# Smaller and later transfers around a streamed weight queue in a one-core Strassen trunk layer

## The chip, the cores and the metric

The kernel runs on one core of one Trainium2 chip. The metric is the device time of one execution in microseconds (us). It is compared as the median of several runs. The engines are TensorE (PE in the profile, its weight loads PEld), VectorE (DVE), ScalarE (ACT), GpSimd (POOL) and the queue engine SyncE (SP). DMA transfers are asked for from two places only, SP and POOL, and all run on the core's 16 DMA engines.

## The reference

One layer of a streaming encoder over 4096 tokens of width 1024, with a memory of 256 rows. Shortened:

```
h    = rms_norm(x, pre_norm)                      # x: (1, 4096, 1024)
proj = h @ w_in                                   # 1024 -> 3072 (b, c, u) + 1536 (gate) + 512 (mq)
z    = c * u;  mix = b * conv3(z)                 # causal convolution over time, 3 taps
k, v = split(rms_norm(mem, mem_norm) @ w_mem_kv)  # 256 memory rows, 4 heads of 128
mem_o = softmax(mq @ k.T / sqrt(128)) @ v
y    = (concat([mix, mem_o]) * silu(gate)) @ w_out
out  = x + rms_norm(y, post_norm)
```

## The kernel before

All arithmetic is fp32. Each fp32 operand is split in a high and a low part, and each product is three matmuls (hi x hi, hi x lo, lo x hi; lines 1701 to 1703), each of 128x128 weights by 512 columns.

**Tiling.** The tokens are 8 tiles of 512 (`NT`), two tiles to a macro (`MACROS` = 4). In a macro TensorE goes through 20 pairs of weight blocks (`PAIRS`), and each pair is multiplied by a Strassen scheme with seven products (`PRODUCTS`, in the order R1, R5, R6, R3, R7, R2, R4). One product is a *unit*: 12 matmuls. A *step* is one product in a macro, `step = 7 * pair + r`, so a macro has 140 steps. What a pair holds is its kind: `q` (memory queries), `m` (gates of the memory branch), and groups `c`, `u`, `b`, `g` of the convolution branch. After the four macros the output projection (`OUT_STEPS`, 16 pairs) follows.

**Weights.** In macro 0 the Strassen sums of weights are built by ACT and DVE in one of four buffers (`slots`, `SLOTS` = 4) and kept in memory on the chip's HBM (`w_split`). In macros 1 to 3 SP loads each unit back (`load_unit`, line 600, 512 KB). SP goes through the steps in order, and `load_unit` for unit u waits until unit u-4 has been multiplied:

```
sp.wait_ge(unit_done, u - SLOTS + 1)
```

So what stands in SP's loop at `now = step - SLOTS` is issued when TensorE has ended a unit that is four units back. Whatever else SP asks for stands behind this load in SP's queue, and ahead of the next.

**Keys and values.** In macro 3, after steps 18, 20, ..., 32 (`KV_AT`), TensorE also multiplies eight key/value blocks, 0 to 7, of two units each. They use the same four slots, so in this stretch "four units back" is two steps and one key/value block back. SP loads a block's raw weights (`load_kv(b)`, line 645, 512 KB) in one of two buffers. In program step 17 + 2b ACT makes the high parts of block b (line 937) and DVE the low parts (line 1357), and TensorE multiplies them after step 18 + 2b.

**Stores and staging.** POOL stores what a pair has made when the whole pair is done (`keep`): queries and SiLU gates as one transfer of 1024 KB, gated convolution outputs as two of 512 KB. Tokens of the next macro come as four halves of 1024 KB (`load_x` after the pairs in `X_AFTER`). In macro 2 (`SUMS_MACRO`) POOL also brings and stores sums of the output weights: rows for the memory part (`memory_rows_in`, two transfers of 512 KB; `memory_rows_out`), and for the convolution part (`out_sums_in`, `out_sums_out`, 1024 KB each). At the end of macro 3 SP loads 1024 KB parts for the output projection (`OUT_X_AT`) and four blocks of 384 KB (`OUT_RAW_AT`).

Of the kernel before, what the change touches and what calls it, by code (L numbers as in the profile page):

```python
# [56 lines left out]
X_AFTER = {2: 0, 3: 2, 4: 1, 5: 3}  # L57
# [15 lines left out]
OUT_X_AT = [122, 123, 124, 125]  # L73
# [114 lines left out]
def trunk(nc, x, x_t, mem, mem_x, in_gains, post_g, conv, w_in, w_kv, w_conv, w_mem, out):  # L188
# [6 lines left out]
    with ExitStack() as ctx:  # L195
# [254 lines left out]
        def mix_free(eng, p, tile):  # L450

            if p == ALL_PAIRS:
                eng.wait_ge(g_kept_dma, 32 * 4 * MACROS)
            else:
                eng.wait_ge(y_final, 2 * (p - ALL_PAIRS) - 1 + tile)
# [56 lines left out]
        def zb_free(eng, p):  # L512

            m = p // PAIRS
            if kind_of(p) == "q":
                if row_of(p) > FIRST_Q:
                    eng.wait_ge(q_kept_dma, 16 * (2 * m + 1))
                elif m < MACROS - 1:
                    eng.wait_ge(tap0_done, 4 * 4 * (m + 1))
                    eng.wait_ge(halo_out, 2 * 4 * (m + 1))  # L520
                else:
                    eng.wait_ge(q_kept_dma, 16 * 2 * m)
            elif row_of(p) > FIRST_C:
                eng.wait_ge(tap0_done, 4 * conv_group(p))
                eng.wait_ge(halo_out, 2 * conv_group(p))
            elif m:
                eng.wait_ge(q_kept_dma, 16 * count("q", p))
            else:
                eng.wait_ge(m_kept_dma, 16 * 2)
# [17 lines left out]
        def load_block(eng, p, x):  # L547

            if (p, x) in WAS:
                raw_used(eng, *WAS[p, x])  # L550
            sub = 2 * (p - ALL_PAIRS) + (x in (X21, X22))
            for h in range(2):
                eng.wait_ge(mem_kept_dma[h], 16 * MH // 2 * (sub // SUB + 1))
            eng.wait_ge(g_kept_dma, 32 * 4 * (sub // (2 * SUB) + 1))
            done = raw_dma[PLACE[p, x]] if p == ALL_PAIRS else block_dma[x]
            eng.dma_start(raw(p, x), flat(g_kept[sub, 1 * (x in (X22, X12))])).then_inc(done, 16)

        @block.sync
        def _(sp):
# [87 lines left out]
            def load_q(n):  # L647
                t, h = divmod(n, MH)
                if n >= 2:
                    sp.wait_ge(q_lo_done, n - 1)  # L650
                else:
                    sp.wait_ge(mw_kept_dma[0], 16 * PRODUCTS)
                sp.wait_ge(q_kept_dma, 16 * 2 * (t // 2 + 1))
                sp.dma_start(q_raw[n % 2], q_kept[t // 2, h, t % 2]).then_inc(q_dma[n % 2], 16)

            def load_m(n):
                t, h = divmod(n, MH)
                if n >= 2:
                    sp.wait_ge(mem_gated, n - 1)
                else:  # L660
                    sp.wait_ge(w_lo, BUILT[KV_UNIT[KV_BLOCKS - 1, 1]] + 1)
                sp.wait_ge(m_kept_dma, 16 * 2 * (t // 2 + 1))
                sp.dma_start(m_raw[n % 2], m_kept[t // 2, h, t % 2]).then_inc(m_dma[n % 2], 16)

            for m in range(1, MACROS):
                for i in range(PAIRS):
                    p = m * PAIRS + i
                    for r in range(PRODUCTS):
# [15 lines left out]
                        if m + 1 < MACROS:  # L684
                            continue
                        if now == 2:
                            sp.wait_ge(hop_lo_done, (m + 1) * PRODUCTS)
                            sp.dma_start(mem_in[:], mem).then_inc(mem_dma, 16)
                        if now == 6:
                            sp.wait_ge(sums_kept_dma, 16 * HK)  # L690
                        if now in (6, 9):
                            load_kv((now - 6) // 3)
                        if now in (12, 14):
                            load_q((now - 12) // 2)
                        if now in KV_AT and KV_AT.index(now) + 2 < KV_BLOCKS:
                            load_kv(KV_AT.index(now) + 2)
                        if now == KV_AT[-1]:
                            load_m(0)
                            load_m(1)
# [19 lines left out]
                        if step == OUT_RAW_AT:  # L719
                            sp.wait_ge(mem_gated, HEADS)  # L720
                            sp.wait_ge(scores_done, HEADS)
                            for x in (X11, X21, X22, X12):
                                load_block(sp, ALL_PAIRS, x)
                    if i in X_AFTER and m + 1 < MACROS:
                        sp.wait_ge(hop_lo_done, (m + 1) * PRODUCTS)
                        load_x(X_AFTER[i], m + 1)
# [21 lines left out]
        def _(pool):  # L748
# [45 lines left out]
            def keep(p):  # L794
                m, i, kind = p // PAIRS, row_of(p), kind_of(p)
                if kind == "q":
                    pool.wait_ge(c12_done, seven_to(p))
                    pool.wait_ge(c22_done, seven_to(p))
                    pool.wait_ge(c11_done, seven_to(p))
                    pool.wait_ge(copied, count("qcy", p) + 1)  # L800
                    pool.dma_start(kept_as(q_kept, m, i - FIRST_Q), zb[:, :, HALO:]).then_inc(q_kept_dma, 16)
                if kind == "m":
                    pool.wait_ge(silu_done, silu_count(p, R4))
                    pool.dma_start(kept_as(m_kept, m, i), zb[:, :, HALO:] if p == 1 else mix[:]).then_inc(m_kept_dma, 16)
                if kind == "g":
                    group = (i - FIRST_C) // 4
                    pool.wait_ge(gated, 4 * (count("g", p) + 1))
                    for f in range(2):
                        pool.dma_start(g_kept[2 * SUB * m:2 * SUB * (m + 1), group // 2, :, group % 2 * 2 + f, :].rearrange("s p n -> p s n"),
                                       flat(mix[:, 2 * f:2 * f + 2, :]).rearrange("p (s n) -> p s n", n=P)).then_inc(g_kept_dma, 16)  # L810
# [7 lines left out]
            def out_sums_in(k):  # L818

                if k:  # L820
                    pool.wait_ge(sums_kept_dma, 16 * k)
                else:
                    pool.wait_ge(mw_lo, HB * PRODUCTS)
                for tile in range(2):
                    pool.dma_start(out_sums[:, 2 * tile:2 * tile + 2, :], w_conv[tile, :, k:KT:HK, :]).then_inc(out_raw_dma, 16)

            def out_sums_out(k):
                pool.wait_ge(out_sum_done, 4 * (k + 1))
                pool.dma_start(sums_kept[:, :, k, :].rearrange("s p n -> p s n"), out_sums).then_inc(sums_kept_dma, 16)

            def memory_rows_in(k):
# [5 lines left out]
                for tile in range(2):  # L837
                    pool.dma_start(out_sums[:, 2 * tile:2 * tile + 2, :], w_mem[tile, :, k:MH:HB, :]).then_inc(mw_raw_dma, 16)
# [5 lines left out]
            for p in range((MACROS - 1) * PAIRS):  # L844
                m, i = divmod(p, PAIRS)
                if m == SUMS_MACRO and i == 0:
                    memory_rows_in(0)
                for step in range(PRODUCTS * i, PRODUCTS * (i + 1)):
                    if m == SUMS_MACRO and step in MW_AT:
                        memory_rows_out(MW_AT.index(step))  # L850
                        if MW_AT.index(step) == PRODUCTS - 1:
                            memory_rows_in(1)
                    rows(m, step)
                keep(p)
                if m == SUMS_MACRO and i in SUMS_AFTER:
                    k = SUMS_AFTER.index(i)
                    if k:
                        out_sums_out(k - 1)
                    if k < HK:
                        out_sums_in(k)  # L860
            for step in range(PAIRS * PRODUCTS):
                p, r = divmod(step, PRODUCTS)
                if r == R5 and p:
                    keep((MACROS - 1) * PAIRS + p - 1)
# [3 lines left out]
            keep(ALL_PAIRS - 1)  # L868
# [37 lines left out]
        def _(act):  # L906
# [78 lines left out]
            def evacuate(p, r):  # L985
# [37 lines left out]
                if kind in "mg" and r in (R3, R7, R2, R4):  # L1023
                    if kind == "m":
                        if r == R3:
                            act.wait_ge(m_kept_dma, 16 * count("m", p))
                            act.wait_ge(g_kept_dma, 32 * count("g", p))
# [208 lines left out]
        def _(dve):  # L1236
# [13 lines left out]
            def norm(tile, k):  # L1250
                if tile < 2:
                    dve.wait_ge(spread_done, tile + 1)
                else:
                    dve.wait_ge(rs_wide_dma, 16 * (tile - 1))
                    dve.wait_ge(x_dma[tile % 2 + 2 * (k // HK)], 16 * (tile // 2 + 1))
# [185 lines left out]
            def convolve(p, n):  # L1441
# [16 lines left out]
                if n == 0:  # L1458
                    if group % 4 == 0:
                        dve.wait_ge(m_kept_dma, 16 * count("m", p))  # L1460
                    if group:
                        dve.wait_ge(g_kept_dma, 32 * group)
# [62 lines left out]
            def memory(p, r, step):  # L1525
                if 13 <= step < 15:
                    dve.wait_ge(rs_wide_dma, 16 * (NT - 1))
                    dve.wait_ge(mem_dma, 16)
# [402 lines left out]
```

## Time and profile before

| | |
|---|---|
| median of three runs | 2178.57 us (2177.86 to 2178.81) |
| the profiled execution | 2178.16 us, its span 2176.3 us |
| TensorE (PE) busy | 2152.8 us, 99% |
| VectorE busy | 1209.7 us, 56% |
| ScalarE busy | 745.6 us, 34% |
| GpSimd busy | 174.7 us, 8% |
| DMA | 550.33 MB, mean 253 GB/s |

The profiled execution takes 1.9 us more than its span, and lies 0.4 us below the median of the three runs. By time, macro 0 runs to about 398 us, macro 1 to about 790, macro 2 to about 1185, macro 3 to about 1706, and the output projection to the end. Busy shares say that TensorE is the engine that matters; what is left to find is in its waits.

### The profile page before, as it was taken

How to read it: one execution, taken by the hardware profiler on the slowest of the kernel's cores; microseconds unless marked ns; L12 is line 12 of the kernel's file. 1: busy time of each engine (PE TensorE's matmuls, PEld its weight loads, DVE VectorE, ACT ScalarE, POOL GpSimd, SP SyncE). 2: the span in 40 equal slices, each digit the busy share in tenths (PEclk: the TensorE clock that was granted, in tenths of full speed). 3: DMA queues.
4: the chain of work that ended last, by engine and by line, in shares of the span. 5: the costliest groups of instructions: out<-in, count | busy, mean ns of one | idle time of the engine just before them, and what ended most of it. 6: DMA issues, size and time to landing. Idle time of an engine off the chain costs nothing.

```text
span 2176.3 us, 26536 instructions
## 1 busy us (share of the span) xinstructions
PE 2152.8 (99%) x9820; PEld 1782.1 (82%) x9820; DVE 1209.7 (56%) x1819; ACT 745.6 (34%) x1312; POOL 174.7 (8%) x285
## 2 busy tenths in 40 slices
PE   8999999999999999999999999999999999999998
PEld 7888888888888888788887888888887788888887
DVE  7668767643335353354345237576764755566665
ACT  5444333411221342221123233545351633333333
POOL 0000000000000000111100000101010111111110
PEclk9999999999999999999999999999999999999999
DMA  6897777678766778987877765656667866666665
GB/s 242 306 339 277 274 268 269 244 252 274 243 217 217 267 263 307 335 287 265 295 233 257 247 226 190 223 193 218 198 204 291 337 252 240 238 232 227 247 228 193
DMA packets 157103, 550.33 MB, mean 253 GB/s; under 512 B 18032, under 2 KB 18064, under 8 KB 153904
## 3 DMA queue, kind: packets, MB, share of 16 engines
q1 hardware_dynamic: 122048, 416.34, 54.9%
q0 software_dynamic: 34928, 132.30, 17.3%
q8 instruction: 79, 1.29, 0.2%
q14 instruction: 48, 0.39, 0.1%
HBM read 404.90 MB, written 143.67 MB: 252 GB/s over the span
## 4 chain that ended last, share of the span: by engine, by line
PE 89%; DMA 4%; DVE 4%; ACT 1%; issue 1%; SPq 0%; DVEq 0%; ACTq 0%
PE banks L1701 29%; PE banks L1703 29%; PE banks L1702 29%; DMA slots<-w_split 3%; PE banks L1818 1%; DVE hop_lo L1307 1%; DVE x_in L1275 1%; ACT hop_hi L983 1%; ACT probs L1074 0%; DMA mw_stream<-mw_kept 0%; DMA raws<-in_w_in 0%; DMA raws<-in_w_kv 0%; DVE rmax L1483 0%; DVE pt_lo L1498 0%; DVE mix L1467 0%
## 5 line engine op out<-in xcount | busy, mean ns | idle before, releaser
L1701 PE MATMUL banks<-hop_hi,slots 128*128 128x512 f32 x2184 | 853.1, 391 | 8.3 <-DMA slots<-w_split 8.0
L1702 PE MATMUL banks<-hop_lo,slots 128*128 128x512 f32 x2184 | 850.4, 389 | 0.0
L1703 PE MATMUL banks<-hop_hi,slots 128*128 128x512 f32 x2184 | 850.0, 389 | 0.0
L1701 PEld LDWEIGHTS banks<-hop_hi,slots 128*128 128x128 f32 x2184 | 410.1, 188 | 97.3 <-DMA slots<-w_split 13.2
L1703 PEld LDWEIGHTS banks<-hop_hi,slots 128*128 128x128 f32 x2184 | 409.9, 188 | 86.1
L1702 PEld LDWEIGHTS banks<-hop_lo,slots 128*128 128x128 f32 x2184 | 410.1, 188 | 83.1
L1703 PE MATMUL banks<-hop_hi,out_slot 128*128 128x512 f32 x448 | 175.4, 392 | 0.0
L1701 PE MATMUL banks<-hop_hi,out_slot 128*128 128x512 f32 x448 | 175.3, 391 | 0.0
L1702 PE MATMUL banks<-hop_lo,out_slot 128*128 128x512 f32 x448 | 175.2, 391 | 0.0
L1357 DVE TENSOR_TENSOR out_slot<-out_raws,out_slot 128x768 fp32r<-128x768 f32 x112 | 107.3, 958 | 90.3 <-ACT out_slot L937 90.3
L1414 DVE TENSOR_TENSOR u<-banks,u 128x512 f32<-128x512 f32 x54 | 37.3, 691 | 210.5 <-PE banks L1703 210.5
L937 ACT ACTIVATE out_slot<-out_raws 128x768 fp32r<-128x768 f32 x112 | 94.3, 842 | 147.1 <-PE banks L1703 80.4
L1008 ACT ACTIVATE s<-banks 128x512 f32<-128x512 f32 x78 | 46.7, 598 | 263.1 <-PE banks L1703 263.1
L1357 DVE TENSOR_TENSOR slots<-raws,slots 128x512 fp32r<-128x512 f32 x76 | 51.7, 690 | 85.8 <-ACT slots L937 85.8
L1702 PEld LDWEIGHTS banks<-hop_lo,out_slot 128*128 128x128 f32 x448 | 84.1, 188 | 18.6
L1701 PEld LDWEIGHTS banks<-hop_hi,out_slot 128*128 128x128 f32 x448 | 84.1, 188 | 18.7 <-DVE out_slot L1357 0.3
L1703 PEld LDWEIGHTS banks<-hop_hi,out_slot 128*128 128x128 f32 x448 | 84.1, 188 | 18.5
L1016 ACT ACTIVATE u<-banks 128x512 f32<-128x512 f32 x78 | 46.6, 598 | 134.2 <-PE banks L1703 134.2
L1012 ACT ACTIVATE p<-banks 128x512 f32<-128x512 f32 x78 | 46.6, 598 | 124.5 <-PE banks L1703 124.5
L1307 DVE TENSOR_TENSOR hop_lo<-x_in,hop_hi 128x2048 fp32r<-128x2048 f32 x29 | 66.0, 2290 | 27.2 <-ACT hop_hi L983 27.1
L937 ACT ACTIVATE slots<-st_w 128x512 fp32r<-128x512 f32 x80 | 50.1, 626 | 70.6 <-PE banks L1703 51.3
L1357 DVE TENSOR_TENSOR slots<-st_w,slots 128x512 fp32r<-128x512 f32 x80 | 55.1, 689 | 30.9 <-ACT slots L937 30.5
(188 smaller groups left out, 2602.1 us busy)
## 6 DMA issues: line engine op xcount, KB each, us to landing
slots<-w_split SPq DMA_DIRECT2D x406, 512.0 KB, 4.2
w_split<-slots SPq DMA_DIRECT2D x140, 512.0 KB, 3.5
mw_stream<-mw_kept SPq DMA_DIRECT2D x96, 512.0 KB, 4.5
out_raws<-g_kept POOLq DMA_DIRECT2D x60, 384.0 KB, 6.1
raws<-in_w_in SPq DMA_DIRECT2D x86, 256.0 KB, 4.5
x_in<-in_x_t SPq DMA_DIRECT2D x16, 1024.0 KB, 8.2
g_kept<-mix POOLq DMA_DIRECT2D x32, 512.0 KB, 6.9
x_res<-in_x POOLq DMA_DIRECT2D x32, 512.0 KB, 5.3
```

Of the source, the lines that this page charges most:

```text
L937: nc.scalar.activation(dst, src, ACT.Copy).then_inc(w_hi, 1)
L983: nc.scalar.activation(hop_hi[:, r, :, :], (OUT_OF if m == OUT else Y_OF)[r], ACT.Copy).then_inc(hop_hi_done, 1)
L1008: nc.scalar.activation(temp(p, R2), a, ACT.Copy).then_inc(s1_done, 1)
L1012: nc.scalar.activation(temp(p, R7), bank_x, ACT.Copy).then_inc(p5_done, 1)
L1016: nc.scalar.activation(temp(p, R3), a, ACT.Copy).then_inc(u2_done, 1)
L1275: nc.vector.tensor_tensor(dst, a, b, ALU.subtract).then_inc(t_made, 1)
L1307: nc.vector.tensor_tensor(hop_lo[:, r, :, :], (OUT_OF if m == OUT else Y_OF)[r], hop_hi[:, r, :, :].bitcast(f32), ALU.subtract).then_inc(h ...
L1357: nc.vector.tensor_tensor(lo, src, hi.bitcast(f32), ALU.subtract).then_inc(w_lo, 1)
L1414: nc.vector.tensor_tensor(dst, src, temp(p, r), ALU.add).then_inc(done, 1)
L1701: nc.tensor.matmul(dst, a, c, start=first, stop=False, skip_group_check=True)
L1702: nc.tensor.matmul(dst, a, d, start=False, stop=False, skip_group_check=True)
L1703: return nc.tensor.matmul(dst, b, c, start=False, stop=last, skip_group_check=True)
```

## The change

Every transfer that was made in one or two large parts is made in smaller ones, and several are asked for at other steps:

- `keep` becomes `keep_block`: queries, gates and outputs are stored block by block (256 KB each) as soon as a block is ready. The counts in waits on these stores go from 16 or 32 to 64 a pair.
- Tokens come as 16 quarters of 256 KB, one every fourth step from step 16 to step 76 (`X_QUARTERS`), instead of four halves.
- The memory input comes as four parts at `now` = 7 to 10 instead of one at `now` = 2.
- Key/value blocks 0 and 1 are asked for at `now` = 11 and 13 instead of 6 and 9, and each of the others one `now` later than before.
- The first memory rows are asked for at the end of macro 1 (`ROWS_AT`) and each pair of such transfers is split over two steps. Sums are stored in four parts.
- The parts for the output projection are asked for at steps 122, 124, 127 and 131 (before 122 to 125), and its four blocks at 126, 129, 133 and 135 (before all at 127).

The diff, cut to its core:

```
-X_AFTER = {2: 0, 3: 2, 4: 1, 5: 3}
+X_QUARTERS = {16 + 4 * q: ((0, 2, 1, 3)[q // HK], q % HK) for q in range(4 * HK)}
-OUT_X_AT = [122, 123, 124, 125]
+OUT_X_AT = [122, 124, 127, 131]
+OUT_BLOCKS_AT = [126, 129, 133, 135]
-SUMS_AT = [PRODUCTS * i + 13 for i in SUMS_AFTER[:HK]]
+SUMS_AT = [PRODUCTS * i + 15 for i in SUMS_AFTER[:HK]]
+ROWS_AT = [127, 131]
-OUT_RAW_AT = 127
+MEM_AT = (7, 8, 9, 10)
...
+            def load_x_quarter(n, q, m):
+                tile, k = n % 2, n // 2 * HK + q
+                sp.dma_start(x_in[:, tile, k, :], x_t[2 * m + tile][:, k, :]).then_inc(x_dma[n], 16)
...
-                if r == R4 and p in X_AFTER:
+                if PRODUCTS * p + r in X_QUARTERS:
                     sp.wait_ge(hop_lo_done, PRODUCTS)
-                    load_x(X_AFTER[p], 1)
+                    load_x_quarter(*X_QUARTERS[PRODUCTS * p + r], 1)
...
-                        if now == 2:
+                        if now in MEM_AT:
                             sp.wait_ge(hop_lo_done, (m + 1) * PRODUCTS)
-                            sp.dma_start(mem_in[:], mem).then_inc(mem_dma, 16)
-                        if now == 6:
-                            sp.wait_ge(sums_kept_dma, 16 * HK)
-                        if now in (6, 9):
-                            load_kv((now - 6) // 3)
+                            two = slice(2 * MEM_AT.index(now), 2 * MEM_AT.index(now) + 2)
+                            sp.dma_start(mem_in[:, two, :], mem[:, two, :]).then_inc(mem_dma, 16)
+                        if now == 11:
+                            sp.wait_ge(sums_kept_dma, 64 * HK)
+                        if now in (11, 13):
+                            load_kv((now - 11) // 2)
...
-                        if now in KV_AT and KV_AT.index(now) + 2 < KV_BLOCKS:
-                            load_kv(KV_AT.index(now) + 2)
-                        if now == KV_AT[-1]:
+                        if now - 1 in KV_AT and KV_AT.index(now - 1) + 2 < KV_BLOCKS:
+                            load_kv(KV_AT.index(now - 1) + 2)
+                        if now - 1 == KV_AT[-1]:
                             load_m(0)
                             load_m(1)
...
+            def keep_block(p, r):
+
+                m, i, kind, n = p // PAIRS, row_of(p), kind_of(p), OF[r]
+                f, t = divmod(n, 2)
                 if kind == "q":
...
+                    pool.dma_start(q_kept[m, 2 * (i - FIRST_Q) + f, t], zb[:, n, HALO:]).then_inc(q_kept_dma, 16)
```

On SP, in the key/value stage of macro 3, the rows before are these (`st_w<-q_kept` are the first two query loads, `slots<-w_split` the streamed units, `raws<-in_w_kv` key/value blocks; the first one here is block 2):

```order
L654 DMA st_w<-q_kept 128x512
L600 DMA slots<-w_split 128x1024 x4
L645 DMA raws<-in_w_kv 128x1024
L600 DMA slots<-w_split 128x1024 x2
L645 DMA raws<-in_w_kv 128x1024
```

and now:

```order
L660 DMA st_w<-q_kept 128x512
L606 DMA slots<-w_split 128x1024 x5
L651 DMA raws<-in_w_kv 128x1024
L606 DMA slots<-w_split 128x1024 x2
L651 DMA raws<-in_w_kv 128x1024
```

Block 2 stands behind five streamed units since the query load instead of four, and the later blocks keep this shift, since two units stand between each two of them in both.

On POOL, at the change from macro 1 to macro 2, the rows before are these (`in_w_mem` are the memory rows, `row` the token rows for the norm):

```order
L801 DMA q_kept<-zb 128x4x512 x2
L838 DMA raws<-in_w_mem 128x2x512 x2
L804 DMA m_kept<-mix 128x4x512 x2
L764 DMA row<-in_x 128x1024
L842 DMA mw_kept<-mw_split_98 128x1024
```

and now:

```order
L859 DMA raws<-in_w_mem 128x2x512
L809 DMA q_kept<-zb 128x512 x2
L859 DMA raws<-in_w_mem 128x2x512
L809 DMA q_kept<-zb 128x512 x6
L812 DMA m_kept<-mix 128x512 x8
L770 DMA row<-in_x 128x1024
```

The memory rows moved ahead of nearly all query stores, and a store of 1024 KB became four.

On POOL, in the middle of macro 2 (the seventh memory row leaves, the second set comes in), the rows before:

```order
L842 DMA mw_kept<-mw_split_99 128x1024
L842 DMA mw_kept<-mw_split_98 128x1024
L838 DMA raws<-in_w_mem 128x2x512 x2
L764 DMA row<-in_x 128x1024
L842 DMA mw_kept<-mw_split_99 128x1024
```

and now:

```order
L863 DMA mw_kept<-mw_split_99 128x1024
L863 DMA mw_kept<-mw_split_98 128x1024
L859 DMA raws<-in_w_mem 128x2x512 x2
L770 DMA row<-in_x 128x1024
L863 DMA mw_kept<-mw_split_99 128x1024
```

Here the order is the same: the two steps between the halves hold no other work of POOL.

## Rows read from the trace of the kernel before

**Rows 1.** The page, busy time of each engine.

```profile
PE 2152.8 (99%) x9820; PEld 1782.1 (82%) x9820; DVE 1209.7 (56%) x1819; ACT 745.6 (34%) x1312; POOL 174.7 (8%) x285
```

**Rows 2.** Waits of PE: us in total, times, longest.

```profile
PE banks L1701 <- DMA slots<-w_split: 8.0, 9, 1.6
...
PE banks L1701 <- DMA mw_stream<-mw_kept: 0.9, 1, 0.9
```

**Rows 3.** Waits of PE in macro 2, 790 to 1185 us.

```profile
PE banks L1701 <- DMA slots<-w_split: 4.5, 5, 1.6
```

**Rows 4.** Waits of PE early in macro 3, 1185 to 1300 us.

```profile
PE banks L1701 <- DMA slots<-w_split: 2.0, 2, 1.5
PE banks L1701 <- DVE slots L1357: 1.1, 2, 0.9
```

**Rows 5.** Waits of PE at the end of macro 3, 1660 to 1706 us.

```profile
PE banks L1701 <- DMA slots<-w_split: 1.5, 2, 0.7
```

**Rows 6.** Chain that ended last, 780 to 900 us: start, us, what.

```profile
789.39 9.38 DMA slots<-w_split
...
889.22 8.14 DMA slots<-w_split
```

**Rows 7.** Timeline of POOL, 784 to 792 us: start, us, engine, line.

```profile
787.97 0.75 POOL L801 DMA_DIRECT2D q_kept<-zb  x1 [18.42 <-DVE zb L1414]
788.71 1.42 POOL L838 DMA_DIRECT2D raws<-in_w_mem  x2
```

**Rows 8.** Timeline of POOL, 884 to 890 us.

```profile
886.18 0.53 POOL L842 DMA_DIRECT2D mw_kept<-mw_split  x1 [6.90 <-DVE mw_split L1302]
886.71 1.45 POOL L838 DMA_DIRECT2D raws<-in_w_mem  x2
```

**Rows 9.** Waits of the SP queue, 1180 to 1190 us.

```profile
SPq L688 <- DVE hop_lo L1307: 5.8, 1, 5.8
```

**Rows 10.** Timeline of SP in the key/value stage, 1236 to 1245.6 us.

```profile
1236.18 0.32 SPq L600 DMA_DIRECT2D slots<-w_split  x1
1236.55 0.43 SPq L645 DMA_DIRECT2D raws<-in_w_kv  x1
1242.10 3.04 SPq L600 DMA_DIRECT2D slots<-w_split  x2
1245.18 0.43 SPq L645 DMA_DIRECT2D raws<-in_w_kv  x1
```

**Rows 11.** Timeline of PE, 1244.3 to 1244.9 us: the start of block 2.

```profile
1244.40 0.39 PE L1703 MATMUL banks<-hop_hi,slots 128*128 128x512 f32 x1
1244.62 0.28 PE L1701 MATMUL banks<-mem_hi,slots 128*128 128x256 f32 x1
```

**Rows 12.** DMA to landing: four key/value blocks (1236 to 1262 us); all streamed units.

```profile
DMA to landing us min/median/max: 4.1/5.1/5.7
...
DMA to landing us min/median/max: 2.6/4.1/10.2
```

**Rows 13.** Chain that ended last, 1262 to 1280 us: block 6.

```profile
1270.33 8.04 DMA raws<-in_w_kv
1278.40 0.64 ACT slots L937
1279.06 0.70 DVE slots L1357
1279.81 0.50 PE banks L1701
```

**Rows 14.** Stretches at the end: busy us (x) by engine, PEclk, DMA share, GB/s.

```profile
2170.50:2174.00 3.50, 0.00 (x0) 0.00 (x0) 2.86 (x5) 0.85 (x3) 0.54 (x1) 1.00 0.39 156
2174.00:2176.30 2.30, 0.00 (x0) 0.00 (x0) 0.00 (x0) 0.00 (x0) 0.00 (x0) 0.50 0.60 223
```

**Rows 15.** The stretch 1664 to 1672 us, columns as in rows 14.

```profile
1664.00:1672.00 8.00, 7.25 (x31) 5.66 (x31) 6.13 (x14) 0.60 (x1) 0.00 (x0) 1.00 1.03 406
```

**Rows 16.** Timelines of SP and DVE in macro 0, 56 to 75 us.

```profile
58.56 1.36 SPq L565 DMA_DIRECT2D raws<-in_w_in  x2
...
64.71 2.29 DVE L1307 TENSOR_TENSOR hop_lo<-x_in,hop_hi 128x2048 fp32r<-128x2048 f32 x1 [2.13 <-ACT hop_hi L983]
...
73.76 0.68 DVE L1351 TENSOR_TENSOR st_w<-raws 128x512 f32<-128x512 f32 x1
```

More of the change, by code:

```diff
@@ L718, in _ @@
                             load_stream(0, R5)
-                        if step == OUT_RAW_AT:
+                        if step in OUT_BLOCKS_AT:
                             sp.wait_ge(mem_gated, HEADS)
                             sp.wait_ge(scores_done, HEADS)
[L722 to L726, printed above, removed]
+                            load_block(sp, ALL_PAIRS, (X11, X21, X22, X12)[OUT_BLOCKS_AT.index(step)])
             for r in (R6, R3, R7, R2, R4):
@@ L808, in keep @@
-                    for f in range(2):
-                        pool.dma_start(g_kept[2 * SUB * m:2 * SUB * (m + 1), group // 2, :, group % 2 * 2 + f, :].rearrange("s p n -> p s n"),
-                                       flat(mix[:, 2 * f:2 * f + 2, :]).rearrange("p (s n) -> p s n", n=P)).then_inc(g_kept_dma, 16)
+                    pool.wait_ge(gated, 4 * count("g", p) + ORDER_OF[r])
+                    pool.dma_start(g_kept[SUB * (2 * m + t):SUB * (2 * m + t + 1), group // 2, :, group % 2 * 2 + f, :].rearrange("s p n -> p s n"),
+                                   mix[:, n, :].rearrange("p (s n) -> p s n", n=P)).then_inc(g_kept_dma, 16)
@@ L812, in keep_gated, with keep_first, keep @@
+            def keep_first(p):
+                for r in (R3, R7, R2, R4):
+                    keep_block(p, r)
+            def keep(p, r):
+                if p >= DIRECT and kind_of(p) in "qm" and r in (R3, R7, R2, R4):
+                    keep_block(p, r)
+                if kind_of(p) == "g" and r in (R7, R2, R4):
+                    keep_block(p, {R7: R3, R2: R7, R4: R2}[r])
+                if p and kind_of(p - 1) == "g" and r == R1:
+                    keep_block(p - 1, R4)
             def keep_gated(n):
@@ L845, in _ @@
                 m, i = divmod(p, PAIRS)
[L846 to L848 removed]
+                for r in range(PRODUCTS):
+                    step = PRODUCTS * i + r
+                    if m + 1 == SUMS_MACRO and step in ROWS_AT:
+                        memory_rows_in(0, ROWS_AT.index(step))
                     if m == SUMS_MACRO and step in MW_AT:
                         memory_rows_out(MW_AT.index(step))
[L851 to L852 removed]
+                    for tile in range(2):
+                        if m == SUMS_MACRO and step == MW_AT[PRODUCTS - 1] + 2 * tile:
+                            memory_rows_in(1, tile)
                     rows(m, step)
[L854 to L860, printed above, removed]
+                    keep(p, r)
+                    if m == SUMS_MACRO and i - 1 in SUMS_AFTER[:HK] and r in (R6, R7):
+                        out_sums_in(SUMS_AFTER.index(i - 1), int(r == R7))
+                    if m == SUMS_MACRO:
+                        for k, first in enumerate(SUMS_AT):
+                            if first < step <= first + 4:
+                                out_sums_out(k, step - first - 1)
+                if p < DIRECT:
+                    keep_first(p)
             for step in range(PAIRS * PRODUCTS):
                 p, r = divmod(step, PRODUCTS)
[L863 to L864 removed]
+                keep((MACROS - 1) * PAIRS + p, r)
                 for n in range(HEADS):
@@ L1459, in convolve @@
                     if group % 4 == 0:
-                        dve.wait_ge(m_kept_dma, 16 * count("m", p))
+                        dve.wait_ge(m_kept_dma, 64 * count("m", p))
                     if group:
-                        dve.wait_ge(g_kept_dma, 32 * group)
+                        dve.wait_ge(g_kept_dma, 64 * group)
                 w = conv_w[:, j, :]
```

64 lines of the change are left out of this document (31 added, 33 removed).

## The prediction

> **What bounds the kernel now.** I read the busy times first [rows 1]: TensorE is busy for 2152.8 of 2176.3 us, so no transfer matters until it makes TensorE wait, and everything that could be won is 23.5 us. Next I read TensorE's waits [rows 2]: the only large group is on streamed units that landed late, nine times and 8.0 us. By stretches, five of these (4.5 us) are in macro 2, two (2.0 us) early in macro 3 with two waits on key/value parts (1.1 us) beside them, and two (1.5 us) at the end of macro 3 [rows 3 to 5]. Macros 0 and 1 have none. A wait costs a little more than its idle time: SP's loads follow the units, and two of them start 3.04 - 0.32 = 2.72 us apart [rows 10], so 12 matmuls take 2.72 us, 0.23 each, while the view draws each 0.39 long [rows 11]. So 0.16 us goes on top of each idle time. The nine waits cost about 8.0 + 9 x 0.16 = 9.4 us.
>
> Then the chain shows what a wait is made of. A streamed unit is asked for when the unit four back has ended, so it has three units, 3 x 2.72 = 8.16 us, to land. In most cases it takes 4.1 us; in the two cases of [rows 6] it took 9.38 and 8.14. The first was asked for at 789.39, just behind a 1024 KB query store and with two 512 KB memory rows [rows 7]. So the waits are bursts: about 2 MB of other transfers asked for within two microseconds.
>
> **The change part by part.**
>
> Stores block by block, tokens in quarters, memory rows earlier. In macro 2 the five waits cost 4.5 + 5 x 0.16 = 5.3 us. The burst at 788 us comes apart: its memory rows go ahead of the query stores, a step or more apart, and each store is a quarter of what it was. I count its wait as gone, and those behind the other large stores and the 1024 KB token halves too. One burst stays whole: at 886 us a memory row leaves and two 512 KB parts come in behind it [rows 8]. Nothing stands between the two parts in POOL's order, so splitting them over two steps does not part them. The unit asked for behind them took 8.14 us [rows 6]. I leave 1.0 us for this and for what stays near 956 us (one of the two sum loads is still asked for there), so this part gives 4.3 us, between 3 and 5.3.
>
> The price of more transfers: POOL gets 24 + 24 + 32 + 12 = 92 more (queries 8 to 32, gates 8 to 32, gated outputs 32 to 64, sums 4 to 16). At no more than the 0.75 us that the 1024 KB store took [rows 7] that is 69 us more on an engine that is busy for 174.7 [rows 1] and idle around them: nothing on the path.
>
> Here a rule speaks against the change. The trace has 1024 KB stores ahead of the worst landings [rows 6, 7]. The Trainium skill, "DMA: Bandwidth & Descriptors", section Bandwidth, says to batch transfers to at least 1 MiB; it gives 341 GB/s at 1 MB and 138 at 64 KB. By it each part of 256 KB would hold the DMA engines longer per byte, and the gain above would be eaten in part. By the rows it is not the engines' time but the size of a burst that makes a unit late, and the sum goes by that.
>
> The memory input at `now` = 7 to 10. Before, SP stood at `now` = 2 for 5.8 us until the last operand of the macro was split [rows 9], and the next streamed unit was asked for late. At `now` = 7 the operand is long done. This wait goes, and so, I count, does the other of the two early in macro 3, where a gate store of 1024 KB was under way: 2.0 + 2 x 0.16 = 2.3 us.
>
> The output parts at 122, 124, 127, 131. Four transfers of 1024 KB behind four units of 512 KB asked for 1.5 MB per 2.72 us, 560 GB/s, where the DMA engines moved 406 at full share [rows 15]. Spaced by two or more units it is 375 GB/s or less. I take 1.6 of the 1.5 + 2 x 0.16 = 1.8 us.
>
> In macro 0 the first quarter (step 16) puts SP behind the last operand of the macro: that operand's low part ends at 67.0 us, and two raw weight parts that SP asked for at 58.56 and after stand behind the wait [rows 16]. They would be asked for at about 67.9 and land some 4.5 us later, at 72.4; the sum that reads raw weights runs at 73.76 [rows 16]. It is covered by about one microsecond, and TensorE is four units behind that sum. Nothing; at worst 2 us.
>
> **The key/value blocks, which cost.** Blocks 2 to 7 are asked for one streamed unit later. In SP's order block 2 stands behind five units instead of four. Before, SP asked for it at 1236.55, at the end of step 20; TensorE then had block 1, step 21 and step 22 ahead, and began block 2 at 1244.62 [rows 10, 11]. The next streamed unit was asked for at 1242.10, when step 21 ended. The block now stands behind that one: 1242.10 + 0.36 = 1242.46 (the distance of the two issues before, 1236.18 and 1236.55). That leaves 1244.62 - 1242.46 = 2.16 us. It needs its landing plus the way through ACT and DVE: for block 6 from the landing at 1270.33 + 8.04 = 1278.37 to TensorE at 1279.81, 1.44 us [rows 13]. So TensorE waits for
>
> landing + 1.44 - 2.16 = landing - 0.72 us, once for each block.
>
> Four of these blocks landed in 4.1 to 5.7 us, median 5.1 [rows 12]. In the new place there is less in the queue: the streamed unit before last was asked for 5.9 us earlier and not 2.7 us [rows 10], and the gate stores beside them are quarters. I take 4.3, near the shortest. Each block waits 3.6 us. Six blocks have this place (blocks 0 and 1 are asked for five steps or more ahead): 6 x 3.6 = 21.6 us, between 6 x 3.4 = 20.4 (landing 4.1) and 6 x 4.4 = 26.4 (landing 5.1). In exchange the two waits on key/value parts go, 1.1 + 2 x 0.16 = 1.4 us. Queued behind the waiting conversions are ACT's and DVE's readings of the next unit's bank; they run while the block itself is multiplied, about 3 us (1242.10 - 1236.18 - 2.72 = 3.2, a short wait included [rows 10]), and add nothing.
>
> **The sum**, against the profiled execution: 2178.16 - 4.3 - 2.3 - 1.6 - 1.4 + 21.6 = 2190.2. The median of the runs was 0.4 above the profiled one: 2190.5 us. That is 0.55% slower; a measurement of this kernel can tell about 0.2%, 4.4 us.
>
> **The rivals.**
>
> - *Faster: the later request is hidden.* If the blocks landed in time, only the gains are left: 2178.6 - 9.6 = 2169.0 us. For the sum to break even a block may wait 9.6 / 6 = 1.6 us, so it would have to land in 2.3 us. The shortest landing of all 406 streamed units of this size was 2.6 [rows 12], and a block has one of them right ahead of it. Chance 5%, half of it for the middle (about 2178).
> - *The waits also cost clock.* TensorE stands for more than 3 us six times. At the end of the kernel its granted clock was still full for 3.5 us without a matmul, and half after that [rows 14]; a wait of 3.6 is at that edge, one of 4.4 beyond it. If after each wait the block's own 3 us ran at 1.2 instead of 2.4 GHz, that is 6 x 3 = 18 us more: 2208. The Trainium skill, "TensorE: Matmul & The Clock Gate", Part 1, says that the clock falls to 1.2 GHz after an idle window; by that rule waits of this length may each fall on either side. Chance 8% that it costs most of this, and some of it is in the upper end of the range.
> - *The gains do not come.* The small transfers make as much wait in macro 2 as the large ones (the 886 us burst grows, the rest only moves), and the blocks land in 5.1 us. 2178.6 + 26.4 - 4 = 2201. Chance 10%; half gains, 2195, is within my range.
> - *The change moves nothing that counts*, 2178: it would need both the blocks hidden and the bursts unchanged. 2%.
>
> **How the numbers follow.** The forecast, 2187 to 2196, has 75%. Low end: landing 4.1, all of 5.3 + 2.3 + 1.8 + 1.4 gained, 2178.6 + 20.4 - 10.8 = 2188; a landing of 3.8 takes off 1.8: 2186. High end: landing 5.1 and 5 us of gains give 2200. Range 2186 to 2200. Faster by over 0.2%: 3%. Within: 4%. Slower: 93%.
>
> **What would show it.** Right: TensorE waits on VectorE's parts of key/value blocks (the two waits of 1.1 us become about six of 3.4 us idle, 20 us), the blocks asked for right behind the first streamed unit after a block, waits on streamed units down from nine to three or four, SP's 5.8 us gone, none of the 9 us landings. Wrong: key/value blocks asked for before step 21 ends or landing in under 3 us; new waits on streamed units; a granted clock below full in macro 3; or TensorE waiting in macro 0.

## The result, and the profile after

The changed kernel takes 2204.26 us (2203.04 to 2204.91, four runs) where the kernel before takes 2178.25 beside it: a ratio of 1.0111, with a 95% interval of 1.0091 to 1.0131. It is 26 us slower. The sign was forecast, the size was not: the forecast was 12 us (2190.5, at most 2200). Two executions of versions further down, one of 5618 us and one of 3086 us, were in a slower state and are left out of the medians.

The waits of TensorE in the changed kernel (line, what was waited for, us in total, times, longest), which answer to [rows 2]:

```profile
PE banks L1725 <- DVE slots L1381: 22.0, 6, 4.1
...
PE banks L1725 <- DMA slots<-w_split: 3.0, 4, 1.4
...
PE banks L1725 <- DMA mw_stream<-mw_kept: 1.6, 1, 1.6
```

Six new waits on VectorE's half of a key/value block, 22.0 us idle, stand where two of 1.1 us stood [rows 4]. Counted from the start of the last matmul before to the start of the first after, less the 0.23 us that lie between any two, they are 23.0 us; this is what "from start to start" means below. Waits on streamed units went from nine to four and from 8.0 to 3.0 us. So the waits account for some 15 us of loss, and 26 were measured. The rest is in the granted clock. Stretches around the first of the new waits (us, busy us and instructions by engine, PEclk, DMA share, GB/s):

```profile
1242.60:1246.50 3.90, 0.00 (x0) 0.00 (x0) 0.71 (x2) 1.37 (x3) 0.00 (x0) 1.00 0.71 285
1246.60:1247.10 0.50, 0.47 (x4) 0.50 (x5) 0.49 (x1) 0.16 (x1) 0.00 (x0) 1.00 0.00 0
1247.20:1250.50 3.30, 3.30 (x18) 3.30 (x17) 0.00 (x0) 0.00 (x0) 0.00 (x0) 0.50 0.00 0
1250.60:1256.20 5.60, 5.60 (x28) 4.73 (x28) 0.42 (x1) 0.98 (x2) 0.00 (x0) 1.00 0.20 61
```

TensorE stood for 3.9 us at full clock (2.4 GHz), worked for half a microsecond, and only then got half the clock (1.2 GHz) for 3.3 us, in which it did 18 matmuls of 256 columns (the clock is the column behind the engines, 1.00 for full and 0.50 for half). Over the whole stage, the same columns for both kernels, before and after:

```profile
1225.00:1330.00 105.00, 103.36 (x531) 87.16 (x530) 42.61 (x79) 35.46 (x80) 3.01 (x4) 1.00 0.62 209
```

```profile
1225.00:1360.00 135.00, 112.56 (x526) 93.91 (x527) 42.22 (x79) 35.53 (x81) 5.32 (x9) 0.92 0.47 162
```

In the changed kernel about the same number of matmuls took 30 us more, and the mean clock over 135 us was 0.92: 0.08 x 135 = about 11 us of full-speed work were not granted (the clock is rounded to a hundredth; matmul by matmul it is 9.7, below). This view prices the clock without following a single matmul. It must not be added to the busy column, which already contains it: busy time rose from 103.4 to 112.6 us for as many matmuls, which is the same loss seen from the other side.

How a block came to be late, from the chain of the changed kernel at the first of the six (start, us, what):

```profile
1239.86 0.32 SPq L606
1240.22 4.88 DMA raws<-in_w_kv
1245.13 0.64 ACT slots L961
1245.79 0.70 DVE slots L1381
```

The request is 0.36 us behind the streamed unit's, as forecast; it landed in 4.9 us (the six: 4.3 to 4.9), and TensorE started at 1246.63. Landing - 0.72 gives 4.2 us, and 4.24 is the distance above the regular one from the last matmul before to the first after.

The same matmul in both traces shows where the time goes: the changed kernel is 1.9 us behind at 45 us, 2.1 behind at 790, 2.7 *ahead* at 1220, 28.5 behind at 1310, 26.1 at 1706, and 26.8 at the end. So macro 2 and the start of macro 3 gained 4.8 us, the end of macro 3 gained 2.4, the output projection lost 0.7, and the key/value stage lost 31.2.

### The profile page after: what moved, and what is told of

Read it like the earlier page. It is cut to its first block, busy times and chain, and to the rows that moved or that the text cites. A ratio compares the mean times of both kernels' runs of the same rounds, so it can differ in the third digit from the quotient of the medians.

```text
span 2203.1 us, 26654 instructions
## 1 busy us (share of the span) xinstructions
PE 2162.8 (98%) x9820; PEld 1792.1 (81%) x9820; DVE 1209.7 (55%) x1819; ACT 747.1 (34%) x1312; POOL 223.0 (10%) x377
## 4 chain that ended last, share of the span: by engine, by line
PE 91%; DMA 4%; DVE 3%; ACT 1%; issue 1%; SPq 0%; DVEq 0%; ACTq 0%
PE banks L1725 30%; PE banks L1727 30%; PE banks L1726 30%; DMA slots<-w_split 2%; DMA raws<-in_w_kv 1%; PE banks L1842 1%; DVE hop_lo L1331 1%; DMA mw_stream<-mw_kept 0%; ACT probs L1098 0%; DMA raws<-in_w_in 0%; DVE rmax L1507 0%; DVE x_in L1299 0%; DVE pt_lo L1522 0%; DVE slots L1381 0%; ACT hop_hi L1007 0%
## 5 line engine op out<-in xcount | busy, mean ns | idle before, releaser
L816 POOL DMA_DIRECT2D g_kept<-mix x64 | 48.4, 758 | 426.6 <-DVE mix L1463 424.0
```

Source lines behind the costliest of these rows:

```text
L816: pool.dma_start(g_kept[SUB * (2 * m + t):SUB * (2 * m + t + 1), group // 2, :, group % 2 * 2 + f, :].rearrange("s p n -> p s n"), mix[:, ...
```

## Experiments: is it the key/value request, and is it the clock?

**One thing undone.** Everything of the change stays, only blocks 2 to 7 are asked for as before.

```
-                        if now - 1 in KV_AT and KV_AT.index(now - 1) + 2 < KV_BLOCKS:
-                            load_kv(KV_AT.index(now - 1) + 2)
+                        if now in KV_AT and KV_AT.index(now) + 2 < KV_BLOCKS:
+                            load_kv(KV_AT.index(now) + 2)
```

> The changed kernel with one thing undone: key/value blocks 2 to 7 are asked for at the step at which the kernel before asks for them. Theory A (the later request is the whole loss: six waits that cost 23.0 us and, after each, a stretch at half clock worth about 1.6 us, and all else in the change gains about 5 us): the six waits and the low clock in macro 3 go, and the time is 2171 to 2174 us, below the kernel before. Rival B (the many small transfers cost time too, and the key/value waits only hide it): 2178 us or more. Rival C (the low clock comes from something else in the change): the clock still falls in macro 3, and the time is about 2182.

Measured: 2171.15 us, ratio 0.9966 (0.9953 to 0.9979), 7 us below the kernel before and 33 below the changed one. In its waits none on a key/value block is left, and the clock in the stage is full (the stretch 1225 to 1330 us below). One stretch at half clock is left elsewhere in this trace, at 1713 us behind a wait of 1.8 us for the first streamed memory rows.

```profile
1225.00:1330.00 105.00, 104.73 (x535) 88.37 (x534) 47.80 (x93) 36.55 (x83) 5.52 (x9) 1.00 0.62 208
```

One request, one step later, turned a version that is faster by 0.3% into one that is slower by 1.1%.

**The one thing alone.** The kernel before with only the two lines of the opposite edit.

```
-                        if now in KV_AT and KV_AT.index(now) + 2 < KV_BLOCKS:
-                            load_kv(KV_AT.index(now) + 2)
+                        if now - 1 in KV_AT and KV_AT.index(now - 1) + 2 < KV_BLOCKS:
+                            load_kv(KV_AT.index(now - 1) + 2)
```

> The kernel before with only the later request for key/value blocks 2 to 7. Theory A: six waits near 3.8 us and six stretches at half clock, 2178.3 + 23 + 9.7 - 1.4 (two short waits replaced) = 2209.6 us. Rival B: part of the 31 us in this stretch needs the other edits, so it is under 2203. With the gate stores still at 1024 KB two of the six waits should be longer by a microsecond or so.

Measured: 2209.30 us, ratio 1.0160 (1.0125 to 1.0195), against 2209.6 expected. The six waits and the clock of 0.92 are there:

```profile
1225.00:1360.00 135.00, 112.45 (x524) 93.58 (x523) 41.09 (x74) 34.15 (x73) 3.00 (x4) 0.92 0.46 160
```

By the same matmuls its stage lost 30.8 us, where the changed kernel's lost 31.2; its trace also lost 1.7 us at the start, in code that this edit does not touch, and had one more stretch at half clock, behind a streamed unit at 887 us. So the agreement to 0.3 us is in part luck; that of the stage is not. Of its six waits two are longer than in the changed kernel (4.3 and 4.0 against 4.0 and 3.7), the others equal or a little shorter, none by the microsecond that was expected with the large gate stores. The small stores are not what set the landing.

**Filling the waits.** The changed kernel with work of no use on TensorE in front of each late block. The added matmuls write a free bank, and nothing reads them.

```
                         if step in KV_AT:
+                            if KV_AT.index(step) >= 2:
+                                for _ in range(13):
+                                    nc.tensor.matmul(psum[:, 4, :], hop_hi[:, R3, 0, 0:P], hop_hi[:, R3, 0, :], start=True, stop=True)
                             keys_values(KV_AT.index(step))
```

> The changed kernel with 13 more matmuls (2.9 us, into a free bank, results unused) on TensorE just before it waits for each of key/value blocks 2 to 7. They fit in the waits, so the blocks start no later. If the waits alone set the time, it stays at 2204. Theory A: TensorE idles under 1 us each time, the clock stays full, and the six stretches at half clock, 9.7 us in all, are given back: about 2194.5 us. If the half clock has no price it stays at 2204.

Measured: 2196.64 us, ratio 1.0090 (1.0066 to 1.0115): 78 matmuls more, 7.6 us less. The blocks start as late as ever: with the added matmuls left out, the six distances from start to start are 22.7 us, against 23.0. What is given back is clock. Its stage:

```profile
1225.00:1345.00 120.00, 115.69 (x578) 96.38 (x577) 37.60 (x70) 32.27 (x70) 5.51 (x10) 1.00 0.50 173
```

By the medians 2 us of the 9.7 expected did not come, but in the stage all of it did: by the same matmuls the stage lost 21.2 us here and 31.2 in the changed kernel, 10.0 less. So the 2 us lie outside the stage, and where is not shown: the profiled execution is the longest of the four (2208.5 us) and lost 13 us in the output projection, so it doesn't stand for the others there.

**A shorter real wait.** The changed kernel with the late block asked for in front of the streamed unit of that moment.

```
+                            early = step - SLOTS - 1
+                            if m + 1 == MACROS and early in KV_AT and KV_AT.index(early) + 2 < KV_BLOCKS:
+                                sp.wait_ge(unit_done, UNIT_OF[p, r] - SLOTS + 1)
+                                load_kv(KV_AT.index(early) + 2)
                             load_unit(p, r)
...
-                        if now - 1 in KV_AT and KV_AT.index(now - 1) + 2 < KV_BLOCKS:
-                            load_kv(KV_AT.index(now - 1) + 2)
```

> The changed kernel, blocks 2 to 7 still asked for when the step after the block two before has ended, but ahead of the streamed unit of that moment instead of behind it. Each block lands sooner by the 0.36 us of the issue and about 1.3 us of 512 KB not in front of it, so a wait is about 2.2 us instead of 3.8. Theory A (the clock falls for the long wait, not for the fact of waiting): it stays full, and the time is 2204.3 - 9.7 - 6 x 1.6 = about 2185 us. If the clock falls all the same, about 2195. If the landing does not depend on what stands in front of it in the queue, 2202 or more.

Measured: 2190.63 us, ratio 1.0054 (1.0039 to 1.0069), between the forecast of theory A (2185) and the case that the clock falls all the same (2195). The waits:

```profile
PE banks L1727 <- DVE slots L1383: 14.1, 6, 2.4
```

Six waits of 2.4 to 2.6 us from start to start: the blocks landed in 3.5 to 3.7 us instead of 4.3 to 4.9, and were asked for 0.4 us sooner. But the clock did not stay full, nor did it always fall. The first two of these waits and what came after each:

```profile
1240.30:1242.40 2.10, 0.00 (x0) 0.00 (x0) 0.65 (x2) 1.31 (x3) 0.00 (x0) 1.00 1.01 398
1243.10:1246.40 3.30, 3.30 (x18) 3.30 (x17) 0.00 (x0) 0.00 (x0) 0.00 (x0) 0.50 0.01 4
1252.70:1254.80 2.10, 0.00 (x0) 0.00 (x0) 0.65 (x2) 1.15 (x2) 0.00 (x0) 1.00 1.03 419
1255.00:1258.00 3.00, 3.00 (x25) 3.00 (x26) 1.04 (x2) 0.63 (x1) 0.54 (x1) 1.00 0.13 51
```

Two waits of the same length, one followed by 18 matmuls in 3.3 us at half clock and one by 25 in 3.0 at full. Three of the six were followed by such a stretch. The sum closes with it: 7.9 us less waiting and about half of the clock's loss, 13 us, against the 13.6 measured (13.1 in the stage by the same matmuls). Theory A was wrong on this point: it is not only the long wait that costs clock.

**The same idle time, made by filling.** Six instead of 13 added matmuls in the changed kernel.

```
-                                for _ in range(13):
+                                for _ in range(6):
```

> The changed kernel with 6 more matmuls (1.36 us) before the wait for each of key/value blocks 2 to 7 instead of 13. TensorE then stands 2.2 to 2.9 us each time, as in the version that asked for the blocks ahead of the streamed unit, where three of six such waits were followed by a stretch at half clock; the blocks start as late as in the changed kernel. Theory (the clock falls by how long TensorE has just stood and when, not by how late the block is): two to four stretches at half clock in macro 3 instead of six, 2204.3 - 2 to 4 x 1.6 = 2198 to 2201 us. Rival (any wait that the changed kernel has is enough): six, 2204.

Measured: 2203.67 us, ratio 1.0107 (1.0072 to 1.0141): as slow as the changed kernel, nearer to the rival than to the theory. Its profiled execution is the fastest of the four at 2199.57, with four stretches at half clock in the stage; by the same matmuls it lost 27.2 us in the stage, 4.0 less than the changed kernel. Its mean clock over the run was 0.996, that of the other three 0.994, which is also where the changed kernel lies with its six in the stage and one at the start. So it is likely that these three lost clock more often than four times; how often, and where, is not shown.

**The shorter wait, filled.** The version with the block in front, and 8 added matmuls.

```
+                            if KV_AT.index(step) >= 2:
+                                for _ in range(8):
+                                    nc.tensor.matmul(psum[:, 4, :], hop_hi[:, R3, 0, 0:P], hop_hi[:, R3, 0, :], start=True, stop=True)
```

> The version that asks for blocks 2 to 7 ahead of the streamed unit, with 8 more matmuls (1.8 us) before each block. The waits of about 2.5 us shrink to 0.7 us for TensorE. Theory: no stretch at half clock in macro 3, three times 1.6 us given back: 2190.6 - 4.8 = 2185.8 us. Rival (the half clock there came from elsewhere): 2190.6.

Measured: 2186.74 us, ratio 1.0027 (1.0009 to 1.0045), where 2185.8 was expected on a chip on which the kernel before ran 1.5 us slower (2179.87). No stretch at half clock is left in the stage, which lost 13.8 us by the same matmuls, where the version without the added ones lost 18.1:

```profile
1225.00:1335.00 110.00, 106.39 (x532) 88.67 (x531) 35.16 (x65) 31.86 (x69) 5.20 (x9) 1.00 0.52 183
```

## Experiments: where the gain of the rest comes from

Each of these is the kernel before with one part of the change. On this chip the kernel before ran at 2180.32 us, spread from 2175 to 2190, so one or two microseconds can't be told by the clock on the wall; the waits can.

**Stores block by block** (`keep` replaced by `keep_block`, counts of 16 and 32 replaced by 64):

```
-                    pool.dma_start(kept_as(q_kept, m, i - FIRST_Q), zb[:, :, HALO:]).then_inc(q_kept_dma, 16)
+                    pool.dma_start(q_kept[m, 2 * (i - FIRST_Q) + f, t], zb[:, n, HALO:]).then_inc(q_kept_dma, 16)
```

> The kernel before with only the stores of queries, gates and gated outputs made block by block (256 KB instead of 1024 or 512 KB). Theory A (a unit is late when about 2 MB of other transfers is asked for at once): of the waits on streamed units those behind a query or gate store (789, 829 us) and behind a gated output store with other transfers (1064 us) go or shrink below 0.5 us, about 2.5 us gained, and the wait of 1.1 us on key/value block 6, asked for behind a 1024 KB gate store, goes too: about 2174.5 us. Rival (more and smaller transfers cost as much as they save): 2178 or more.

Measured: 2177.29 us, ratio 0.9984 (0.9967 to 1.0001), which can't decide between the two. The waits can, for theory A: those in macro 2 went from 4.5 [rows 3] to 1.9 us, and on block 6 one of 0.2 us is left; the view of macro 2, then of 1185 to 1300 us:

```profile
PE banks L1717 <- DMA slots<-w_split: 1.9, 3, 1.1
```

```profile
PE banks L1717 <- DMA slots<-w_split: 2.4, 1, 2.4
PE banks L1717 <- DVE slots L1373: 0.2, 1, 0.2
```

The second view also shows a loss: SP's stand for the memory input, not part of this edit, now costs 2.4 us idle instead of 1.5, and a stretch at half clock followed it at 1193 us.

**Tokens in quarters** (`X_QUARTERS` and `load_x_quarter`):

```
-X_AFTER = {2: 0, 3: 2, 4: 1, 5: 3}
+X_QUARTERS = {16 + 4 * q: ((0, 2, 1, 3)[q // HK], q % HK) for q in range(4 * HK)}
```

> The kernel before with only the tokens asked for in 16 quarters instead of four halves. Theory A: the longest wait of macro 2 (1.8 us, the unit asked for at 876 us right behind a 1024 KB half) goes, the others stay: 2176 to 2177 us. The macro 0 wait of SP for its first quarter costs TensorE nothing. Rival: the quarters only spread the same lateness over more units, no change, 2178.

Measured: 2176.96 us, ratio 0.9987 (0.9971 to 1.0004). The wait behind the token half (1.8 us at 884 us) is gone, smaller ones remain, 2.1 us idle in place of 4.5:

```profile
PE banks L1705 <- DMA slots<-w_split: 2.1, 5, 0.6
```

**Loads for the output projection apart** (`OUT_X_AT`, `OUT_BLOCKS_AT`):

```
-OUT_X_AT = [122, 123, 124, 125]
+OUT_X_AT = [122, 124, 127, 131]
+OUT_BLOCKS_AT = [126, 129, 133, 135]
```

> The kernel before with only the spacing of the loads for the output projection at the end of macro 3. Theory A: the two waits at 1667 and 1673 us go, 1.8 us or a little more: about 2176 us. Rival: the last of these loads now runs beside those of the next stage, and the first streamed memory rows of the output projection come later: the wait there grows from 1.1 us by as much, no gain.

Measured: 2177.60 us, ratio 0.9982 (0.9963 to 1.0001). No wait of TensorE is left between 1660 and 1706 us, against 1.5 us in [rows 5], and the same matmul at 1706 us is 2.4 us earlier relative to 1660. The wait at the first streamed memory rows stayed at 1.1 us from start to start, so the rival fell.

**Memory input in parts, later** (`MEM_AT`):

```
-                        if now == 2:
+                        if now in MEM_AT:
```

> The kernel before with only the memory input in four parts at the later steps. Theory A: SP no longer stands 5.8 us for the last operand, the wait at 1192 us (1.6 us) goes: about 2176.7 us. Rival: the 1024 KB now compete with key/value block 1 and the query store there, and another unit is late: no change.

Measured: 2181.81 us, ratio 0.9994 (0.9976 to 1.0012), no change that can be told. Between 1185 and 1225 us there is no wait of TensorE at all, and SP no longer stands for the operand; the profiled execution is 1.8 us ahead in that stretch. The same execution lost far more, 7.6 us, in the output projection, which this edit does not touch. Differences of that size between executions are why the median says nothing about an edit worth 1.8 us.

**A better version.** The changed kernel with the request undone, and two more edits: the second half of each sum load a step earlier, and the post-norm gains asked for after the first output blocks.

```
-                    if m == SUMS_MACRO and i - 1 in SUMS_AFTER[:HK] and r in (R6, R7):
-                        out_sums_in(SUMS_AFTER.index(i - 1), int(r == R7))
+                    if m == SUMS_MACRO and i - 1 in SUMS_AFTER[:HK] and r in (R6, R3):
+                        out_sums_in(SUMS_AFTER.index(i - 1), int(r == R3))
...
-            pool.dma_start(post_gain[:], post_g).then_inc(post_dma, 16)
...
                 if j == 0:
+                    pool.dma_start(post_gain[:], post_g).then_inc(post_dma, 16)
                     load_residual(0)
```

> The changed kernel with key/value blocks asked for as before, and two more edits: the second half of each sum load one step earlier, off the token row and gated output store that made a unit 1.5 us late at 989 us, and the post-norm gains (512 KB) asked for after the first output blocks and not before them, since the first streamed memory rows of the output projection came 1.7 us late there. Theory: both waits shrink by half or more, and the stretch at half clock behind the second goes: 2168 to 2170 us. Rival (these loads only change places): 2171.

> The changed kernel with key/value blocks asked for as before, once more, to compare the last one with on the same chip and to see how far its waits in macro 2 and at the output projection vary: 2171 us.

Measured together: 2169.57 us, ratio 0.9947 (0.9930 to 0.9964), and for the version without the two edits 2170.67 us, 0.9955 (0.9939 to 0.9971). The two extra edits can't be told from nothing. In the waits the one on the first streamed memory rows is gone (it was 1.7 us from start to start in the version without them), and so is the one at 989 us (1.6 us there), but another streamed unit in macro 2, at 965 us, is now 2.0 us late, so in macro 2 the rival holds in this trace. The view of the version with them begins:

```profile
PE banks L1874 <- POOL ident L762: 3.5, 1, 3.5
PE banks L1725 <- DMA slots<-w_split: 2.5, 2, 2.0
```

Both versions beat both kernels of the case.

## Why the prediction was right in direction and wrong in size

The steps against the profiled execution: 12.0 us were forecast and 26.8 measured.

- **The late request: right, and nearly its size.** Landing - 0.72 us for each of six blocks held to the tenth (4.9 gives 4.2). The landings were 4.3 to 4.9, median 4.5, where 4.3 was taken: 23.0 us for 21.6.
- **The clock: the step that failed.** The forecast gave it nothing, on the argument that "its granted clock was still full for 3.5 us without a matmul, and half after that [rows 14]; a wait of 3.6 is at that edge". The rival with the clock got 8%, priced at 18 us, and "a granted clock below full in macro 3" stood among its signs of being wrong; that sign came. Each of the six waits was followed by half clock for 3.3 us or a little more, and the stage lost 9.7 us by the same matmuls in both traces: 31.2, less 23.0 - 1.5 of waits. The filled version lost 10.0 us less in the stage, 7.6 by the medians. The argument failed on two counts. One idle stretch at the end of a kernel shows one case: from the end of the last matmul to the fall it was 3.7 us there, 2.4 us at the end of the changed kernel, and up to 5.1 in the other traces; and within the kernel the same idle time was followed by half clock in some places and not in others. And in the changed kernel all six falls came 0.3 to 0.7 us after TensorE had begun again, so a clock that is full through the wait says nothing on what follows.
- **The price of a fall** was taken from the wrong thing, the length of the block (3 us each, 18 in all). It is the length of the stretch at half clock: 9 matmuls of 512 columns from 18.4 to 21.7 us in the changed kernel, 16 in the same stretch before, both below.

```profile
18.40:21.70 3.30, 3.30 (x16) 2.74 (x15) 3.30 (x6) 3.30 (x8) 0.00 (x0) 1.00 1.04 403
```

```profile
18.40:21.70 3.30, 3.30 (x9) 2.60 (x8) 3.30 (x6) 3.30 (x7) 0.00 (x0) 0.50 1.03 400
```

- **A term that was not in the sum: 1.9 us at the start.** These two rows lie behind a wait of 2.1 us for the first operand that both kernels have. In the changed kernel's profiled execution a stretch at half clock followed it, before none, and with the request undone none either, with all other edits in. The version with the later request alone, whose start is that of the kernel before, has it too (1.7 us). So it is not the change's: of all 14 traces four have it.
- **Macro 2 and the start of macro 3: right kind, too much in this trace.** 6.6 us were forecast (4.3 and 2.3), 4.8 came. In the other traces that have all of these edits and no others in this stretch it was 3.8 to 7.1, 6.5 with the request undone, so one trace can't tell the size of this term. The burst at 886 us stayed whole, as POOL's order said, and cost 0.8 us. What was missed is a new one: in macro 2 the second half of the first sum load, a token row, a token quarter and the block stores now stand together, and the unit asked for at 981 us was 1.5 us late. It is not late in every execution: with the request undone POOL has the same order there, and the first trace shows no such wait, the second one of 1.6 us. POOL in the changed kernel:

```profile
975.56 0.56 POOL L770 DMA_DIRECT2D row<-in_x  x1 [19.85 <-ACT row L940]
977.17 0.77 POOL L816 DMA_DIRECT2D g_kept<-mix  x1 [1.06 <-DVE mix L1463]
977.93 0.72 POOL L845 DMA_DIRECT2D raws<-in_w_conv  x1
979.88 0.79 POOL L816 DMA_DIRECT2D g_kept<-mix  x1 [1.23 <-DVE mix L1463]
981.89 1.51 POOL L816 DMA_DIRECT2D g_kept<-mix  x2 [1.22 <-issue]
```

- **The end of macro 3: right.** 1.6 us forecast; 2.4 came by the same matmuls. The 0.7 us lost at the first streamed memory rows were not forecast.
- **Macro 0: right.** SP did stand for 9.8 us at its first quarter, and TensorE lost nothing by it.
- **The rule against small transfers** did not bear on the time: POOL's busy time rose from 174.7 to 223.0 us, and with the request undone the small transfers are in a version that is 7 us faster than before. Here the trace and the Trainium skill ("DMA: Bandwidth & Descriptors", Bandwidth) speak of different things: its rule is for the rate of a stream, and what counted here was when one unit of 512 KB landed beside the others.
- **The rule on the clock** ("TensorE: Matmul & The Clock Gate", Part 1: the clock falls to 1.2 GHz after an idle window) was named and weighed too low. The six waits bear out its direction. It alone does not say which of the waits of 2.2 to 2.9 us cost clock: seven of twelve did.

The sum closes: 12.0 forecast + 9.7 clock + 1.4 landings + 1.8 missing in macro 2 + 1.9 start + 0.7 streamed rows + 0.2 in macro 1 - 0.8 at the end of macro 3 = 26.9, against 26.8.

What stays open: why one wait of 2.5 us costs clock and the next does not, and where outside the key/value stage the filled version lost the 2 us that its median lacks.

## What to carry to other kernels

A request "one step later" must be counted against the last step that still covers it: here the block had 8 us and needed under 7, and one step later was 5.9: 2.7 for a unit of TensorE's work and 3.2 for the key/value block that stood between. Where a busy TensorE is made to wait again and again, price the half clock behind each wait with the wait itself (here 1.6 us on top of 3.8). Look for it at the end of the wait and in the stretch after it, and do not take one idle stretch with full clock as the proof that there is none.

## What the runs showed of the hardware

- A stretch at half clock of 3.3 us or a little more, about 1.6 us of lost work, can follow a wait of TensorE. It began up to 0.6 us before the work did again (at 1285.0 in the version with six added matmuls) and up to 1.1 us after (at 1301.1 in the version with the block in front); in the changed kernel always after, by 0.3 to 0.7 us. Half clock came behind all twelve waits of 3.6 to 4.3 us in the changed kernel and in the one with the edit alone, behind three of six of 2.4 to 2.6 us in one kernel and four of six of 2.2 to 2.9 in another, and behind none of the twelve under 1.2 us in the filled ones. Elsewhere in the 14 traces it also came behind one wait of 3.7 us and six of 1.8 to 2.5, while others as long had none, and in four of them behind the wait of about 2 us for the first operand.
- Work of no use made a kernel faster: 78 added matmuls of 512 columns, 2204.3 to 2196.6 us.
- A block of 512 KB asked for 0.4 us in front of a streamed unit instead of behind it made each wait 1.3 us shorter (3.8 to 2.5 us on average): 0.4 us from the earlier request, 0.9 from the landing (4.5 to 3.6, medians).
